# Cross attention by three products of rounded and rest parts, its pairs weighed one step later

## The reference, cut to what matters

```python
def memory_cross_attention(h, mem, mem_g, wq, wkv, wo):
    mn = rms_norm(mem, mem_g)
    q = (h @ wq).reshape(B, S, H, Dh)             # S = 512, H = 4, Dh = 256
    kv = (mn @ wkv).reshape(B, M, 2, H, Dh)       # M = 256
    s = jnp.einsum('bqhd,bkhd->bhqk', q, kv[:, :, 0]).astype(jnp.float32) * (Dh ** -0.5)
    p = jax.nn.softmax(s, axis=-1).astype(h.dtype)
    o = jnp.einsum('bhqk,bkhd->bqhd', p, kv[:, :, 1])
    return o.reshape(B, S, H * Dh) @ wo
```

## Time and profile before

| | |
|---|---|
| median of 3 runs | 1896.66 us (1895.38 to 1897.12) |
| profiled execution, its time | 1893.84 us |
| its span | 1892.1 us |
| granted PE clock, mean | 0.999 |
| PE busy | 1853.3 us, 98% |
| DVE busy | 1153.6 us, 61% |
| ACT busy | 815.8 us, 43% |

### The profile page before, as it was taken

One profiled execution on the slowest core, in us unless ns is written; L12 is line 12 of the kernel. 1 busy time (PEld: TensorE's weight loads), 2 busy tenths in 40 slices (PEclk: granted clock), 3 DMA queues, 4 the chain that ended last, 5 costly groups with the idle time before them and its releaser, 6 DMA issues. The chain is left out here.

```text
span 1892.1 us, 28167 instructions
## 1 busy us (share of the span) xinstructions
PE 1853.3 (98%) x10762; PEld 1583.9 (84%) x10762; DVE 1153.6 (61%) x1647; ACT 815.8 (43%) x1433; POOL 376.5 (20%) x303
## 2 busy tenths in 40 slices
PE   9999999999999999999999999999999999999997
PEld 7785578889889898997889788897888898989897
DVE  6957956643787556667652356625474368847474
ACT  5216855434546253552223521226453355535362
POOL 0430006500022314103320033300200000522221
PEclk9999999999999999999999999999999999999999
DMA  4330014402233332322332032320451123233331
GB/s 165 119 104 23 1 48 144 152 14 83 85 101 96 95 111 82 125 73 79 100 106 73 31 93 90 93 74 26 143 179 56 54 81 100 80 112 100 99 108 49
DMA packets 99060, 167.73 MB, mean 89 GB/s; under 512 B 5633, under 2 KB 32385, under 8 KB 98689
## 3 DMA queue, kind: packets, MB, share of 16 engines
q1 hardware_dynamic: 98944, 166.15, 28.0%
HBM read 164.03 MB, written 2.10 MB: 88 GB/s over the span
## 5 line engine op out<-in xcount | busy, mean ns | idle before, releaser
L1245 DVE TENSOR_TENSOR w_lo<-raw,w_hi 128x1024 fp32r<-128x1024 f32 x256 | 332.6, 1323 | 255.6 <-ACT w_hi L738 254.1
L738 ACT ACTIVATE w_hi<-raw 128x1024 fp32r<-128x1024 f32 x256 | 264.6, 1057 | 353.7 <-PE ps L1919 342.3
L1919 PE MATMUL ps<-act_hi,w_lo 128*128 128x512 f32 x860 | 340.3, 396 | 7.0 <-DVE w_lo L1245 4.2
L1919 PE MATMUL ps<-act_lo,w_hi 128*128 128x512 f32 x864 | 336.1, 390 | 0.0
L1919 PE MATMUL ps<-act_hi,w_hi 128*128 128x512 f32 x860 | 335.0, 390 | 0.0
L1919 PEld LDWEIGHTS ps<-act_hi,w_lo 128*128 128x128 f32 x860 | 161.5, 188 | 45.2 <-DVE w_lo L1245 6.3
L1919 PEld LDWEIGHTS ps<-act_lo,w_hi 128*128 128x128 f32 x864 | 162.3, 188 | 34.9 <-issue 1.9
L1919 PEld LDWEIGHTS ps<-act_hi,w_hi 128*128 128x128 f32 x860 | 161.4, 188 | 34.0
L1919 PE MATMUL ps<-ff_hi,w_lo 128*128 128x512 f32 x448 | 176.6, 394 | 0.0
L1919 PE MATMUL ps<-ff_lo,w_hi 128*128 128x512 f32 x448 | 176.6, 394 | 0.0
L1919 PE MATMUL ps<-ff_hi,w_hi 128*128 128x512 f32 x448 | 176.6, 394 | 0.0
(11 more groups left out here) (252 smaller groups left out, 4024.6 us busy)
## 6 DMA issues: line engine op xcount, KB each, us to landing
raw<-in_db_w_qkv SPq DMA_DIRECT2D x72, 512.0 KB, 3.9
raw<-in_w_up SPq DMA_DIRECT2D x64, 512.0 KB, 3.8
raw<-in_w_down SPq DMA_DIRECT2D x64, 512.0 KB, 3.7
raw<-in_xa_wkv SPq DMA_DIRECT2D x32, 512.0 KB, 3.7
raw<-in_da_w_qkv SPq DMA_DIRECT2D x24, 512.0 KB, 3.9
raw<-in_xa_wq SPq DMA_DIRECT2D x16, 512.0 KB, 3.7
raw<-in_xa_wo SPq DMA_DIRECT2D x16, 512.0 KB, 3.6
raw<-in_da_w_o SPq DMA_DIRECT2D x8, 512.0 KB, 3.9
```

Of the source, the lines that this page charges most:

```text
L738: nc.scalar.activation(w_hi[:, g % 4], raw[:, g % 4], ACT.Copy).then_inc(w_hi_ready, 1)
L1245: nc.vector.tensor_tensor(w_lo[:, g % 4], raw[:, g % 4], w_hi[:, g % 4].bitcast(f32), ALU.subtract).then_inc(w_lo_ready, 1)
L1919: last = nc.tensor.matmul(ps[:, s + m, 0:width], left, right, start=(k == 0 and n == 0 and not early), stop=(k == KT - 1 and n == 2))
```

## The change

Scores and weighing of the cross attention are made of three rounded products like the projections. For that:

- Keys and values (`xk`, `xv`) are split into `_hi` and `_lo` once in a layer: four ACT copies and four DVE subtractions of 128x1024, in the first query unit. They lie on tiles of the memory that are free by then.
- A query goes from PSUM into `stage` or `half`; ACT rounds it to `xq_hi`, and DVE writes `xq_lo`. For queries 0 to 3 the rests stand among the queries, for 4 to 7 they stand in DVE's steps 3 to 6.
- ACT copies the transposed probabilities as rounded `pxT_hi`; DVE, one step later, writes `pxT_lo`. There are two pairs of steps of buffers instead of two steps.
- Two steps are weighed together, in 12 matmuls of 128x256, at t = n + 5 for odd n (before: each step alone at t = n + 4). The output rounding and its rests stand one step later.
- PE's transposes of step n wait for `pxT_lo` of step n-2, where they waited for the copy of that step.
- The first pair of the output projection does its first two banks for both rows first, and waits for the reading of head 2 only before the other two banks.

```diff
@@ ACT, attention step: copy of the transposes @@
-                        if n >= 2:
+                        if a.narrow and n >= 4:
+                            act.wait_ge(a.weighed, 2 * (n // 2) - 2)
+                        elif n >= 2 and not a.narrow:
                             act.wait_ge(a.weighed, n - 1)
+                        elif a.narrow:
+                            nc.scalar.activation(pair_place(pxT_hi, n), a.turned_all(n)..., ACT.Copy).then_inc(a.pT, 1)
...
@@ ACT, query units @@
+                        act.wait_ge(bank_done, 4 * u)
+                        for n in range(4):
+                            source, to, _ = memory_halves(n)
+                            nc.scalar.activation(to, source, ACT.Copy).then_inc(memory_hi, 1)
+
+                def query_head(k):
+                    act.wait_ge(bank_out[(u + k // 4) % 2], banks_out(u + k // 4, k % 4))
+                    nc.scalar.activation(xq_hi[:, k, :], query_place(k), ACT.Copy).then_inc(query_hi, 1)
...
-                unit(u, lambda m: root(f"xpre{layer}") if m == 0 else None, between=last_planned)
-                unit(u + 1, first_steps=(att_x[layer], exp_cross, 2), second=4)
-                attention(att_x[layer], exp_cross, 2, (3, head_split))
+                unit(u, first_queries, between=last_planned)
+                unit(u + 1, lambda m: query_head(4 + m), first_steps=(att_x[layer], exp_cross, 2), second=4)
+                attention(att_x[layer], exp_cross, 2, (4, head_split))
@@ DVE, attention step, after the scaling of step t-1 @@
+                    if a.narrow and 0 <= t - a.lag - 1 < a.n:
+                        n = t - a.lag - 1
+                        dve.wait_ge(a.pT, n + 1)
+                        if n >= 4:
+                            dve.wait_ge(a.weighed, 2 * (n // 2) - 2)
+                        nc.vector.tensor_tensor(pair_place(pxT_lo, n), a.turned_all(n)...,
+                                                pair_place(pxT_hi, n).bitcast(f32), ALU.subtract).then_inc(a.pT_lo, 1)
@@ DVE, query units @@
+                def query_rest(k):
+                    dve.wait_ge(query_hi, KT * layer + k + 1)
+                    nc.vector.tensor_tensor(xq_lo[:, k, :], query_place(k), xq_hi[:, k, :].bitcast(f32),
+                                            ALU.subtract).then_inc(query_lo, 1)
...
-                attention(a, take_max, probs_plain, range(2, a.n + 5), (4, head_rests))
+                attention(a, take_max, probs_plain, range(2, a.n + 6), (5, head_rests), *[(k - 1, late_query(k)) for k in range(4)])
@@ PE, unit @@
+                    order = [(a, range(nb)) for a in range(2)]
+                    if late_banks and j == 0:
+                        order = [(a, banks) for banks in (range(2), range(2, nb)) for a in range(2)]
@@ PE, attention step @@
                         if n > 1:
-                            pe.wait_ge(a.pT, a.copies * (n - 1))
+                            pe.wait_ge(a.pT_lo if a.narrow else a.pT, a.copies * (n - 1))
...
-                    if a.lag < t <= a.n + a.lag:
-                        n = t - a.lag - 1
-                        pe.wait_ge(a.pT, a.copies * (n + 1))
+                    behind = a.lag + 1 + a.narrow
+                    if behind <= t < a.n + behind:
+                        n = t - behind
+                        if a.narrow and n % 2 == 0:
+                            continue
+                        pe.wait_ge(a.pT_lo if a.narrow else a.pT, a.copies * (n + 1))
@@ PE, cross attention @@
-                        last = nc.tensor.matmul(a.narrow_scores(t), xq[:, XB * h + b, s * P:(s + 1) * P],
-                                                xk[:, XB * h + b, :], start=(b == 0), stop=(b == XB - 1))
+                        for p, (left, right) in enumerate(((xq_lo[:, k, c], xk_hi[:, k, :]), (xq_hi[:, k, c], xk_lo[:, k, :]),
+                                                           (xq_hi[:, k, c], xk_hi[:, k, :]))):
...
-                pe.wait_ge(lo_ready, SPLITS[f"xo{layer}"] + XB * (XA_HEADS - 1))
-                unit(xo, act_hi, act_lo, SPLITS[f"xo{layer}"],
-                     before_pair={1: lambda: attention(range(a.n + 1, a.n + 6), *cross)})
+                unit(xo, act_hi, act_lo, SPLITS[f"xo{layer}"], late_banks=third_head_read,
+                     before_pair={1: lambda: attention(range(a.n + 1, a.n + 5), *cross)})
```

More of the change, by code:

```diff
@@ L237, in build @@
             ex_sb = sb("ex_sb", [P, 4, MEM], scope=scope)
-            pxT_sb = sb("pxT_sb", [P, 2, MEM], scope=scope)
+            pxT_hi = sb("pxT_hi", [P, 2, MEM // P, 2 * P], f32r, scope=scope)
+            pxT_lo = sb("pxT_lo", [P, 2, MEM // P, 2 * P], f32r, scope=scope)
         sq = sb("sq", [P, KT, S])
@@ L256, in build @@
             mem_sq = sb("mem_sq", [P, KT, MEM], scope=scope)
+        with ExitStack() as scope:
+            below = sb("below", [P, KT, S], f32r, scope=scope)
+            xk_lo = sb("xk_lo", [P, KT, MEM], f32r, scope=scope)
+            xv_lo = sb("xv_lo", [P, MEM // P, D], f32r, scope=scope)
+            xk_hi = sb("xk_hi", [P, KT, MEM], f32r, scope=scope)
+            xv_hi = sb("xv_hi", [P, MEM // P, D], f32r, scope=scope)
+            xq_lo = sb("xq_lo", [P, KT, S], f32r, scope=scope)
         with ExitStack() as scope:
@@ L392, in __init__ @@
                 self.pT = sem(name + "_pT")
+                self.pT_lo = sem(name + "_pT_lo") if narrow else None
                 self.weighed = sem(name + "_weighed")
@@ L418, in build, with pair_place, query_place, memory_halves @@
         att_x = [Attention(f"cross{i}", XA_HEADS, MEM // P, narrow=True) for i in range(2)]
+        def pair_place(p, n):
+            return p[:, n // 2 % 2, :, (n % 2) * P:(n % 2 + 1) * P]
+        def query_place(k):
+            return stage[:, k % 2, :] if k < 6 else half[:, k % 2, :]
+        def memory_halves(n):
+            if n < 2:
+                return [keys[:, n * HALF:(n + 1) * HALF, :] for keys in (xk, xk_hi, xk_lo)]
+            return [values[:, n - 2, :] for values in (xv, xv_hi, xv_lo)]
         def gcol(layer, name, k):
@@ L1731, in last_planned @@
                         planned(18)
+                        for n in range(4):
+                            source, hi, lo = memory_halves(n)
+                            dve.wait_ge(memory_hi, 4 * layer + n + 1)
+                            nc.vector.tensor_tensor(lo, source, hi.bitcast(f32),
+                                                    ALU.subtract).then_inc(memory_lo, 1)
+                def query_rest(k):
+                    dve.wait_ge(query_hi, KT * layer + k + 1)
+                    nc.vector.tensor_tensor(xq_lo[:, k, :], query_place(k), xq_hi[:, k, :].bitcast(f32),
+                                            ALU.subtract).then_inc(query_lo, 1)
                 u = UNITS[f"xq{layer}"]
@@ L1876, in unit @@
             def unit(u, hi, lo, split, ii=0, split_ii=0, tokens=None, nb=4, width=NB, last_bank=None, before_pair={},
-                     early=False, after=None):
+                     early=False, after=None, late_banks=None):
                 s = 4 * (u % 2)
@@ L1902, in unit @@
                         pe.wait_ge(w_lo_ready, ii * 8 + (4 * u + j + 1))
-                    for a in range(2):
+                    order = [(a, range(nb)) for a in range(2)]
+                    if late_banks and j == 0:
+                        order = [(a, banks) for banks in (range(2), range(2, nb)) for a in range(2)]
+                    for a, banks in order:
                         k = 2 * j + a
                         pe.wait_ge(lo_ready, split_ii * KT + (split + k + 1))
-                        for m in range(nb):
+                        if late_banks and j == 0 and a == 0 and banks[0] == 2:
+                            late_banks()
+                        for m in banks:
                             if last_bank and k == 0 and m == 3 and not early:
@@ L2273, in weigh_cross @@
                     for d in range(XB):
+                        c = slice((XB * h + d) * P, (XB * h + d + 1) * P)
                         for b in range(MEM // P):
-                            c = (XB * h + d) * P
-                            last = nc.tensor.matmul(ps[:, a.cross_bank(XB * h + d), s * P:(s + 1) * P], xv[:, b, c:c + P], p_of(a, n, b),
-                                                    start=(b == 0), stop=(b == MEM // P - 1))
+                            hi, lo = [p[:, n // 2 % 2, b, :] for p in (pxT_hi, pxT_lo)]
+                            for p, (left, right) in enumerate(((xv_lo[:, b, c], hi), (xv_hi[:, b, c], lo), (xv_hi[:, b, c], hi))):
+                                last = nc.tensor.matmul(ps[:, a.cross_bank(XB * h + d), (s - 1) * P:(s + 1) * P], left, right,
+                                                        start=(b == 0 and p == 0), stop=(b == MEM // P - 1 and p == 2))
                     return last
@@ L2291, in cross_starts @@
                 def cross_starts():
-                    for n in range(4):
```

(3 more changed lines are left out.)

44 lines of the change are left out of this document (37 added, 7 removed).

## The result

The changed kernel takes 1899.43 us (median of 17 runs, 1897.95 to 1900.72), the kernel before 1896.05 us in 17 runs beside it (1894.14 to 1898.36). The ratio is 1.0018 with a 95% interval of 1.0011 to 1.0024: 3.4 us slower, just under the 0.2% that I had called no change. Forecast were 1898.2 us and "same". The profiled execution after took 1899.45 us (span 1897.7, mean granted clock 0.996). So the two profiles lie 5.6 us apart, and the medians 3.4.

The account below looks back on a forecast made before the run. PE, busy 98% of the span, was taken as the bound; 5.5 us less PE work a layer was outweighed by waits, +0.75 a layer, 1.5 for two: 1896.66 + 1.5 = 1898.2 us, own range 1896 to 1901, wider range 1893 to 1902.5.

Parts of the forecast that it names:

- Products: Cross-attention scores and weighing on PE: rounded 128x256 matmuls 0.118 us apart, 5.5 us less PE work a layer without waits.
- The gate: Cross-attention loop: PE's transposes wait 0.54 us for `pxT_lo` every second step; 1.47 us from score's end, two steps 3.92.
- The weight pair: Before score 4: ACT rounds it behind queries 4 to 7, score 4 comes 1.48 us later, hole 0.90 to 3.2.
- Steps 5, 6 and 16: PE's waits in the cross-attention loop, for `pxT_lo` or late DVE work: 0.63, 0.71 and 1.25 us.
- `xo`: Start of the output projection after cross attention: the earlier 0.70 us wait goes, as 2.7 us of matmuls cover the reading.
- The rest of the probabilities: DVE's subtraction making `pxT_lo`: taken as 0.42 us, at most 0.68, which would add 1.9 us a layer.
- rival B: Cross-attention loop: DVE becomes the bound as the `pxT_lo` subtraction takes 0.68 us; +5.2 us, 1901.9; chance 0.20.
- Keys and values: Their ACT copies and DVE subtractions hide where DVE idles 10.18 us; costed at nothing, up to 4.8 us a layer uncovered.
- the sum of a layer: Walk through one layer's cross attention to the end of the output projection: 429.56 against 428.81, 0.75 us slower.
- Rival C: Before step 2's maximum: weight pair not in the way, layer ends 1.8 us earlier than forecast; 1894.6 us, chance 0.17.
- the offset: Whole kernel: the median of the runs lies 2.8 us above the profiled execution, added to the forecast for that execution.
- rival A: Cross attention and `xo`: engines overlap, PE never waits more than before; 6.2 us a layer faster, 1884.2, chance 0.08.

Follow-up runs that it names:

- the pair first: Changed kernel with ACT rounding the weight pair ahead of the exponential of step 0 and queries 4 to 7; 1897.25 us, ratio 1.0002 to the kernel before.
- the first experiments: Four variants of the changed kernel, run together on one chip, five rounds each, beside 21 runs of the kernel before (1896.63 us).
- both edits and the copy first: Changed kernel with weight pair ahead of queries, `pxT_lo` subtraction ahead of DVE's maximum, and ACT's `pxT_hi` copy ahead of its exponential; 1887.52 us, ratio 0.9956.
- rest first: Changed kernel with DVE's subtraction for `pxT_lo` of step t-4 put ahead of the maximum of step t; 1895.34 us, ratio 0.9989 to the kernel before.

## Why the prediction was right, and what it missed

Right in value (1899.43 in 1896 to 1901, forecast 1898.2) and, step by step, in mechanism. The value owes something to luck: the change was forecast at +1.5 us and measured at +3.4, and the median of 3 runs from which I started (1896.66) was 0.6 above that of 17 (1896.05). "No change" was forecast below 3.8, which 3.4 meets narrowly. The steps:

- *Products.* 0.118 forecast, 0.119 measured (the row of 11 distances above). With 192 such matmuls a layer this is up to 0.2 us. The estimate of 109 ns from the Trainium skill ("TensorE: Matmul & The Clock Gate", section "Back-to-back issue gap") lies further off.
- *The gate*, the way from a score over DVE to the transposes. Forecast a wait of 0.54 in every second step and 3.92 us for two; measured 0.47 and 3.97. Two errors partly cancel. From the end of a score to the transposes it is 417.03 - 415.46 = 1.57 instead of 1.47. DVE's part is as forecast; PE starts 0.15 behind the end of the subtraction (416.46 + 0.42 = 416.88), not 0.06, which was read behind an ACT instruction. Transposes and weighing take 414.74 - 413.06 = 1.68, where restart, transposes and weighing were put at 0.10 + 0.22 + 1.42 = 1.74. A restart costs a score about 0.10 (in layer 1, 0.82 instead of 0.72), as forecast, but the transposes only 0.03 (0.17 to the next start instead of 0.14).
- *The weight pair.* Forecast 1.7 us of waiting for `w_hi`, measured 1.64. Score 4 was forecast 11.69 us after score 0 (395.50 - 383.81), and came 396.39 - 384.73 = 11.66 after it. The hole itself was forecast at 3.2 us, and measured 2.94. The forecast's own terms give 3.0: the 0.90 of before, 1.48 by which score 4 is later, and the 0.62 that four scores save.
- *Steps 5, 6 and 16.* Forecast waits of 0.63, 0.71 and 1.25; in layer 1, at full clock, they are 0.56, 0.60 and 1.18.
- *`xo`.* No wait at its start, and 2.06 hidden behind the first two banks (forecast 2.1).
- *The rest of the probabilities* takes 0.417 us (median of 32), so rival B had no ground. Keys and values were hidden: DVE is idle 5.11 us behind them, where the earlier trace rows had 10.18.

Mis-sized was the sum of a layer: forecast +0.75 us, measured 46.11 - 44.91 = +1.20 in layer 1. The timeline of that layer says where the 0.45 arise. From score 4 to the transposes of step 6 it took 4.19 instead of 4.09, and from there to those of step 16 it took 19.79 instead of 19.53, the 0.05 a pair of steps from the gate. The other 0.09 is the end of the layer before: the prediction took it as 428.81, and the trace has 428.73, with a layer of 44.91 and not 45.00. The stretches ahead of score 4 and from step 16 on were each forecast to 0.05.

Rival C, which had the weight pair out of the way, was wrong as to this kernel, and right as a price: with the pair first a layer is 1.76 us shorter, for which it had said 1.8.

Missed altogether was the clock. I had read the span of before, with a mean clock of 0.999, as typical, and added the offset to the median without asking what makes the offset. The runs of before beside the first experiments answer that, by the mean granted clock of each run:

| mean clock of the run | runs | mean time us |
|---|---|---|
| 0.999 | 1 | 1893.5 |
| 0.998 | 7 | 1895.1 |
| 0.997 | 5 | 1896.7 |
| 0.996 | 7 | 1898.3 |
| 0.995 | 1 | 1897.8 |

A mean lower by 0.001 is 1.9 us of full clock lost (0.001 x 1895), and the time goes up by 1.6 from each of the first four rows to the next. So most of the spread of this kernel's runs, 6 us, goes with the places at which its clock falls. In the changed kernel it doesn't show (1899.9 us at a mean clock of 0.994, 1899.4 at 0.996), as far as can be seen because its falls in the cross attention lie partly beside waits. The profile after shows two such places that have nothing to do with the change, at 96 to 99 and at 956 to 959 us:

```profile
96.00:98.00 2.00, 2.00 (x6) 1.54 (x6) 2.00 (x2) 0.03 (x1) 1.89 (x1) 0.50 0.12 15
...
956.00:958.00 2.00, 2.00 (x6) 1.58 (x5) 0.00 (x0) 0.00 (x0) 0.00 (x0) 0.51 0.68 243
```

In the profile of before both are at full clock:

```profile
96.00:98.00 2.00, 2.00 (x10) 1.61 (x10) 2.00 (x2) 0.00 (x0) 1.81 (x1) 1.00 0.10 20
...
956.00:958.00 2.00, 2.00 (x11) 1.65 (x10) 0.00 (x0) 0.00 (x0) 0.00 (x0) 1.00 0.02 8
```

Each of the two costs 1.6 us: behind the first the same matmul starts 1.62 us later than in the profile of before, ahead of it 0.04; at the second the difference goes from 2.45 to 4.04. That is the step of the table, so one fall more explains one row. The two profiled executions differ by 5.6 us: cross attention gives 1.80 + 1.20 = 3.0, these two places 3.2, and other differences outside the cross attention take off 0.6. Each of the two was low in 5 of the 9 profiled kernels. Of the medians' 3.4 us, the two layers at full clock make 2 x 1.2 = 2.4, and a fall behind the hole 0.6 more in each layer where it happens. Whether the remaining 0.4 or less is anything can't be told.

Where did the gain go? Products and late banks were worth 6.2 us a layer by rival A. The kernel with both edits and the copy first is 44.91 - 40.31 = 4.6 us shorter a layer than before. The changed kernel gave all of this back to the order of two lists: a weight pair behind four queries on ACT (1.76), and a subtraction behind a maximum on DVE together with the copy behind an exponential on ACT (the rest).

## What to carry to other kernels

When a new operation is put into a software pipeline over several engines, ask of its place in the engine's list what it depends on and what stands ahead of it: an operand that has been ready for a step belongs at the head of the step, ahead of what waits for this step's own data. An idle hole of PE costs more than its length when the clock falls with it: here that came with 5 of 6 holes of 2.94 us, and with none of 1.20. Test two suspected edits together too, since one can hide the other's worth. Before an offset between a profile and a median is carried over, read the mean clock of each.

## What the runs showed of the hardware

- PE's clock fell to half at 5 of 6 idle holes of 2.94 us, for 3.4 us in four of them and for about 7 in the fifth (rest first, layer 1, 1456 to 1463). There it fell while PE was still idle (0.97 at 1454 to 1456, PE's next matmul at 1456.76); in layer 0 of that kernel it fell 1.0 us after PE had started again at 396.76. Why one of the six kept its clock is open.
- The places at 96 and 956 us are not idle. In the changed kernel PE does 16 matmuls of 1x1 for a statistic in 2.9 us ahead of the low clock, and at 96 us the first full ones are already slowed (0.47 apart, where they are 0.23 at full clock); at 956 four run at full clock before. The kernel before does the same 16 (92.87 to 95.78 us) and keeps its clock:

```profile
92.91 2.91 PE L2143 MATMUL ps<-ones,rstd 1*128 1x1 f32 x16
95.75 0.68 PE L2002 MATMUL ps<-act_hi,w_lo 128*128 128x512 f32 x1
96.22 0.63 PE L2002 MATMUL ps<-act_lo,w_hi 128*128 128x512 f32 x1
```

PE counts as busy there, and no run here tried what these matmuls do to the clock.

- An engine's wait can hide part of a low clock: the fall in layer 0 of the changed kernel cost 0.6 us for 3.4 at half clock, and one in dense work, at 96 us, 1.6. In the kernel with the rest first one of 3.4 us cost 0.2 (layer 0), and the one of about 7 us 1.3 (layer 1).
